# RWKV's 64x64 products issued alternately on four quarters of the array, the second head's inverse in the other half of the rows

## The reference

```
def step(S, inp):
    r_t, w_t, k_t, v_t, kk_t, a_t = inp
    sa = jnp.einsum('bhvk,bhk->bhv', S, -kk_t)
    S = (S * w_t[:, :, None, :] + sa[..., None] * (kk_t * a_t)[:, :, None, :]
         + v_t[..., None] * k_t[:, :, None, :])
    y = jnp.einsum('bhvk,bhk->bhv', S, r_t)
    return S, y
```

## Time and profile before

| | |
|---|---|
| median of 3 runs | 4763.44 us (4747.4, 4763.44, 4767.96) |
| the profiled execution | 4764.35 us, its span 4762.1 us |
| TensorE busy | 4174.8 us (88% of the span) |
| weight loads | 2744.4 us (58%) |
| VectorE, ScalarE, POOL busy | 1666.0, 1215.6, 700.7 us |
| mean granted clock of TensorE | 0.928 |

### The profile page before, as it was taken

One profiled execution on the slowest core, in us unless ns is written; L12 is line 12 of the kernel. 1 busy time (PEld: TensorE's weight loads), 2 busy tenths in 40 slices (PEclk: granted clock), 3 DMA queues, 4 the chain that ended last, 5 costly groups with the idle time before them and its releaser, 6 DMA issues. The chain is left out here.

```text
span 4762.1 us, 73074 instructions
## 1 busy us (share of the span) xinstructions
PE 4174.8 (88%) x28756; PEld 2744.4 (58%) x28756; DVE 1666.0 (35%) x2437; ACT 1215.6 (26%) x1719; POOL 700.7 (15%) x554
## 2 busy tenths in 40 slices
PE   6999669999896998599997979878889999999963
PEld 3888557777555886477774545533544444444423
DVE  3454743332233003643433323722341111111127
ACT  1111344342222111444332241611111111111104
POOL 2221012121112220022120110000001000010015
PEclk8999889899998999899998989989899999999985
DMA  6764232221423433222224315210149999999967
GB/s 221 240 198 154 83 119 83 93 68 64 159 89 115 132 115 104 93 87 71 98 66 147 106 49 214 84 47 27 65 185 359 359 354 358 360 362 360 356 242 264
DMA packets 292915, 803.45 MB, mean 169 GB/s; under 512 B 29121, under 2 KB 120770, under 8 KB 256834
## 3 DMA queue, kind: packets, MB, share of 16 engines
q1 hardware_dynamic: 244578, 624.80, 37.8%
q10 hardware_dynamic: 25632, 93.33, 4.9%
q0 software_dynamic: 22464, 81.80, 4.8%
HBM read 631.02 MB, written 168.82 MB: 168 GB/s over the span
## 5 line engine op out<-in xcount | busy, mean ns | idle before, releaser
L457 PE MATMUL ps<-s_proj_hS,s_proj_wS 128*128 128x512 f32 x3216 | 770.5, 402 | 62.9 <-POOL s_proj_wS L347 62.9
L457 PEld LDWEIGHTS ps<-s_proj_hS,s_proj_wS 128*128 128x128 f32 x3216 | 616.5, 192 | 213.1 <-ACT s_proj_wS L407 63.8
L1673 PE MATMUL ps<-gate_h,gate_w 128*128 128x512 f32 x1536 | 417.8, 416 | 2.5 <-ACT s_rw_og L1226 2.5
L3053 PE MATMUL ps<-s_exp_gu,keep_hT 128*128 128x512 f32 x736 | 339.6, 604 | 14.5 <-DMA s_exp_gu<-in_w_gu_dram 12.6
L1673 PEld LDWEIGHTS ps<-gate_h,gate_w 128*128 128x128 f32 x1536 | 284.1, 192 | 103.8 <-issue 42.0
L3037 PE MATMUL ps<-s_exp_wd,s_exp_aT 128*128 128x512 f32 x736 | 332.8, 595 | 1.9 <-ACT s_exp_aT L2963 1.9
L3058 PE MATMUL ps<-s_exp_gu,keep_hT 128*128 128x512 f32 x736 | 330.9, 592 | 0.0
L3003 DVE TENSOR_TENSOR s_exp_sg<-s_exp_sg,ps 128x256 f32<-128x256 f32 x92 | 38.7, 421 | 659.0 <-ACT s_exp_sg L2984 659.0
L1074 POOL TENSOR_TENSOR gate_w<-gate_raw,gate_w 128x512 fp32r<-128x512 f32 x128 | 168.7, 1319 | 652.5 <-ACT gate_w L1221 652.1
L347 POOL TENSOR_TENSOR s_proj_wS<-s_proj_w,s_proj_wS 128x1024 fp32r<-128x1024 f32 x67 | 170.7, 2550 | 572.9 <-ACT s_proj_wS L407 572.9
L2097 PE MATMUL ps<-keep_mix,s_mix_wb 128*128 128x512 f32 x512 | 224.9, 600 | 29.4 <-DMA s_mix_wb<-in_w_branch_rw_dram 28.5
(11 more groups left out here) (448 smaller groups left out, 6064.3 us busy)
## 6 DMA issues: line engine op xcount, KB each, us to landing
s_exp_gu<-in_w_gu_dram SPq DMA_DIRECT2D x184, 1024.0 KB, 10.8
s_exp_wd<-in_w_down_dram SPq DMA_DIRECT2D x92, 1024.0 KB, 8.8
yrow<-keep_hT ACTq DMA_DIRECT2D x92, 512.0 KB, 9.6
keep_mix<-in_w_ada_dram SPq DMA_DIRECT2D x80, 512.0 KB, 6.4
s_proj_w<-in_w_in_dram SPq DMA_DIRECT2D x66, 512.0 KB, 5.3
proj<-s_proj_o ACTq DMA_DIRECT2D x66, 512.0 KB, 2.7
gate_raw<-in_w_in_dram SPq DMA_DIRECT2D x128, 256.0 KB, 2.9
yrow<-keep_xT SPq DMA_DIRECT2D x4, 8192.0 KB, 49.1
```

The costliest lines, as they stand in the source:

```text
L457: mm = pe.matmul(k.ps[:, 6 + half if last else 2 * b + half, :], wS[:, b, x, t, :], hS[:, y, t, half * HALF:(half + 1) * HALF], start=(t = ...
L1673: mm = pe.matmul(k.ps[:, 7, :], wG[:, g % RING, w, t - y * HK, :], hG[:, h, t, :], start=(t == 0 and w + h == 0), stop=(t == KT - 1 and w ...
L3053: mm = pe.matmul(k.ps[:, 2 if u == 0 else 6, :], xT[:, u, t, :], gu[:, u, t, :], start=(t == 0), stop=False)
```

## The change

**The layout.** `cross(e, h)` is `rows(h ^ e)`: for the second head (e = 1) the other half of the partitions. XT, Y and MA of head 1 now lie there. X, LN, MP and ZX stay, so a level reads `rows(h)` and writes `cross(e, h)`, and the update of X and the product with Z read `cross(e, h)` and write `rows(h)`.

**The order.** Where a loop over heads stood outside, it now stands inside, so successive matmuls of `gram`, L, `level`, the update of X, masked scores by values and the product with Z alternate over all four quarters. The update of XT keeps its loops.

**What is added.** XT of head 1 can't start from LN any more, so B by A of that head is computed again into `cross(1, h)` of bank 2 (16 matmuls, semaphore `lx_ready`), after the first copy of X. `turn_a` becomes four 64x64 matmuls by the identity instead of one 128x128 transpose, per block.

**What is moved.** `gram` does both heads at once, Kd's second head too; the sums of the pair before go around it. VectorE copies X of both heads, then XT of both.

The diff, its core:

```diff
+        def cross(e, h):
+
+            return rows(h ^ e)
...
@@ -1453,18 +1456,26 @@
                 at = at_ts[:, n, :] if dst is X else at_st[:, NLV - n, :]
                 dve.copy_predicated(dst[:, e], at.unsqueeze(1).to_broadcast([P, NB, C]), src).then_inc(ready, 1)
 
-            def first_inverse(p, e):
+            def first_x(p, e):
                 dve.wait_ge(eye_ready, p + 1)
                 dve.wait_ge(l_ready, 2 * p + e + 1)
-                dve.wait_ge(pr_taken, 4 * p + e + 1)
                 put(X, 0, e, blocks(2 + e), x_ready)
-                put(XT, 0, e, LN[:, e, :, 0, :], xt_ready)
-
-            def level(p, n, e):
-                if n < NLV - 1:
+
+            def first_xt(p, e):
+                if e == 0:
+                    dve.wait_ge(pr_taken, 4 * p + 1)
+                    put(XT, 0, e, LN[:, e, :, 0, :], xt_ready)
+                else:
+                    dve.wait_ge(lx_ready, p + 1)
+                    put(XT, 0, e, blocks(2), xt_ready)
+
+            def level_x(p, n):
+                for e in range(2 if n < NLV - 1 else 0):
                     dve.wait_ge(dx_ready, (p * (NLV - 1) + n) * 2 + e + 1)
                     dve.wait_ge(x_ready, (p * NLV + n) * 2 + e + 1)
                     put(X, n + 1, e, blocks(4 + e), x_ready)
+
+            def level_xt(p, n, e):
                 dve.wait_ge(dxt_ready, (p * NLV + n) * 2 + e + 1)
                 dve.wait_ge(xt_ready, (p * (NLV + 1) + n) * 2 + e + 1)
                 put(XT, n + 1, e, blocks(2 + e), xt_ready)
@@ -1684,36 +1702,43 @@
                     tr = pe.transpose(k.ps[:, bank + c // 4, (c % 4) * P:(c % 4 + 1) * P], src(c), k.eye[:])
                 tr.then_inc(tr_ready, 1)
 
-            def gram(lhs, e, bank):
+            def gram(lhs, bank):
                 for c in range(NB):
                     for h in range(2):
-                        i = 2 * c + h
-                        mm = pe.matmul(k.ps[rows(h), bank + c // 4, (c % 4) * P:(c % 4 + 1) * P],
-                                       lhs[rows(e), i * C:(i + 1) * C], AR[rows(e), :, i * C:(i + 1) * C],
-                                       start=True, stop=True)
-                mm.then_inc(pr_ready, 1)
+                        for e in range(2):
+                            i = 2 * c + h
+                            mm = pe.matmul(k.ps[rows(h), bank[e] + c // 4, (c % 4) * P:(c % 4 + 1) * P],
+                                           lhs[rows(e), i * C:(i + 1) * C], AR[rows(e), :, i * C:(i + 1) * C],
+                                           start=True, stop=True)
+                            if c == NB - 1 and h:
+                                mm.then_inc(pr_ready, 1)
 
             def level(p, n):
                 for e in range(2):
                     pe.wait_ge(x_ready, (p * NLV + n) * 2 + e + 1)
                     if n:
                         pe.wait_ge(yy_taken, (p * NLV + n - 1) * 2 + e + 1)
-                    for c in range(NB):
-                        for h in range(2):
-                            mm = pe.matmul(k.ps[rows(h), e, c * C:(c + 1) * C], LN[rows(h), e, c, 0, :], X[rows(h), e, c, :],
+                for c in range(NB):
+                    for h in range(2):
+                        for e in range(2):
+                            mm = pe.matmul(k.ps[cross(e, h), e, c * C:(c + 1) * C], LN[rows(h), e, c, 0, :], X[rows(h), e, c, :],
                                            start=True, stop=True)
-                    mm.then_inc(yy_ready, 1)
+                            if c == NB - 1 and h:
+                                mm.then_inc(yy_ready, 1)
 
             def update(p, n):
                 for e in range(2):
                     pe.wait_ge(yy_taken, (p * NLV + n) * 2 + e + 1)
                     pe.wait_ge(xt_ready, (p * (NLV + 1) + n) * 2 + e + 1)
-                    if n < NLV - 1:
-                        for c in range(NB):
-                            for h in range(2):
-                                mm = pe.matmul(k.ps[rows(h), 4 + e, c * C:(c + 1) * C], XT[rows(h), e, c, :], Y[rows(h), e, c, :],
+                if n < NLV - 1:
+                    for c in range(NB):
+                        for h in range(2):
+                            for e in range(2):
+                                mm = pe.matmul(k.ps[rows(h), 4 + e, c * C:(c + 1) * C], XT[cross(e, h), e, c, :], Y[cross(e, h), e, c, :],
                                                start=True, stop=True)
-                        mm.then_inc(dx_ready, 1)
+                                if c == NB - 1 and h:
+                                    mm.then_inc(dx_ready, 1)
+                for e in range(2):
                     for c in range(NB):
                         for h in range(2):
                             mm = pe.matmul(k.ps[rows(h), 2 + e, c * C:(c + 1) * C], Y[rows(h), e, c, :], XT[rows(h), e, c, :],
@@ -1721,7 +1746,11 @@
                     mm.then_inc(dxt_ready, 1)
 
             def turn_a(q, c):
-                tr = pe.transpose(k.ps[:, c // 4, (c % 4) * P:(c % 4 + 1) * P], AR[:, 0, c * P:(c + 1) * P], k.eye[:])
+                for e in range(2):
+                    for h in range(2):
+                        i = 2 * c + h
+                        tr = pe.matmul(k.ps[cross(e, h), e, c * C:(c + 1) * C],
+                                       AR[rows(e), 0, i * C:(i + 1) * C], k.eye[rows(e), rows(e)], start=True, stop=True)
                 if c == NB - 1:
                     tr.then_inc(tr_ready, 1)
 
@@ -1768,35 +1797,43 @@
                     piece(g)
                 pe.wait_ge(ops_ready, p + 1)
                 pe.wait_ge(tr_taken, 4 * p + 2)
-                gram(B, 0, 4)
+                pe.wait_ge(tr_taken, 4 * p + 3)
+                gram(B, (4, 2))
                 if p:
                     means(p - 1, 0)
-                pe.wait_ge(tr_taken, 4 * p + 3)
-                gram(B, 1, 2)
+                if p % 2:
+                    piece(g + 1)
                 if p:
                     means(p - 1, 1)
-                if p % 2:
-                    piece(g + 1)
                 pe.wait_ge(tr_taken, 4 * p + 4)
-                gram(Kd, 0, 0)
+                pe.wait_ge(pr_taken, 4 * p + 1)
+                gram(Kd, (0, 4))
                 pe.wait_ge(pr_taken, 4 * p + 2)
-                for e in range(2):
-                    for c in range(NB):
-                        for h in range(2):
+                for c in range(NB):
+                    for h in range(2):
+                        for e in range(2):
                             i = 2 * c + h
                             mm = pe.matmul(k.ps[rows(h), 2 + e, c * C:(c + 1) * C], AR[rows(e), 0, i * C:(i + 1) * C],
                                            B[rows(e), i * C:(i + 1) * C], start=True, stop=True)
-                    mm.then_inc(l_ready, 1)
+                            if c == NB - 1 and h:
+                                mm.then_inc(l_ready, 1)
                 if p:
                     variances(p - 1, 0)
                 if p % 2:
                     piece(g + 2)
-                gram(Kd, 1, 4)
                 if p:
                     variances(p - 1, 1)
                 if p % 2:
                     piece(g + 3)
+                if p % 2:
                     g += 4
+                pe.wait_ge(x_ready, 2 * p * NLV + 1)
+                for c in range(NB):
+                    for h in range(2):
+                        i = 2 * c + h
+                        mm = pe.matmul(k.ps[cross(1, h), 2, c * C:(c + 1) * C], B[rows(1), i * C:(i + 1) * C], AR[rows(1), 0, i * C:(i + 1) * C],
+                                       start=True, stop=True)
+                mm.then_inc(lx_ready, 1)
                 pe.wait_ge(pr_taken, 4 * p + 3)
                 level(p, 0)
                 bonus_sums(p, 0)
@@ -1828,10 +1865,10 @@
                     pre_rate(p + 1, 0)
                 piece(g + 7)
                 level(p, 4)
-                for e in range(2):
-                    for c in range(NB):
-                        for h in range(2):
-                            mm = pe.matmul(k.ps[rows(h), 4 + e, c * C:(c + 1) * C], MP[rows(h), e, c, 0, :], Vt[rows(h), c, rows(e)],
+                for c in range(NB):
+                    for h in range(2):
+                        for e in range(2):
+                            mm = pe.matmul(k.ps[cross(e, h), 4 + e, c * C:(c + 1) * C], MP[rows(h), e, c, 0, :], Vt[rows(h), c, rows(e)],
                                            start=True, stop=True)
                 mm.then_inc(mv_ready, 1)
                 if more:
@@ -1844,11 +1881,13 @@
                 pe.wait_ge(mv_taken, p + 1)
                 for e in range(2):
                     pe.wait_ge(xt_ready, (p * (NLV + 1) + NLV) * 2 + e + 1)
-                    for c in range(NB):
-                        for h in range(2):
-                            mm = pe.matmul(k.ps[rows(h), 2 * e + c // 4, (c % 4) * P:(c % 4 + 1) * P], XT[rows(h), e, c, :],
```

(43 more changed lines are left out.)

4 lines of the change are left out of this document (2 added, 2 removed).

## The result

| | before | changed |
|---|---|---|
| median (runs of the first comparison) | 4755.42 us (4) | 4637.42 us (4; 4633.3 to 4643.57) |
| ratio to before, 95% interval | | 0.9758 [0.973, 0.9785] |
| again, later | | 0.973 [0.9706, 0.9754], 0.9745 [0.9717, 0.9772] |
| median of pooled runs | 4756.1 us (40) | 4635.0 us (14) |
| the profiled execution; its span | 4764.35; 4762.1 us | 4637.95; 4635.7 us |

The change makes the kernel 2.5% faster, 121 us by the pooled medians. (The 40 runs of the kernel before are those made beside the later experiments.

The account below looks back on a forecast made before the run. TensorE, busy 93%, was taken to bound the two RWKV stages, 1071 us. Gains from four-quarter order, less 3 us for transposes and 3 for instruction stalls, summed to 98 us: 4764.35 to 4666 us, range 4645 to 4714.

Parts of the forecast that it names:

- item 9: Updates, and level 4 with the group behind it: 128 passes may outrun their instructions; 3 us lost, bounds 0 and 15.
- Items 1 to 3: Levels 1 to 4, update of X, masked scores by values: 29.3 to 15.3 ns a pass; gains 28.5, 28.5, 7.1 us.
- Item 4: Product with Z: 3.64 us become 1.83 at 27 ns a pass; gain 14.4 us over 8 groups.
- The doubt about the bank: Levels and masked scores by values might keep 29 ns through same-bank order: 35.6 us less gain, 4702 us, chance 0.16.
- nothing overlaps: Old order within a level: passes alternate on two quarters writing one PSUM bank, at 29.3 ns each, without overlap.
- Item 5: Gram phase of the four odd pairs, with gate pieces: gain 4.1 us each after 0.5 off for shape changes, 16.4 in all.
- Item 6: Gram phase of even pairs, without pieces: pair 0 gains 0, pair 2 gains 3.1 in layer 1, 6 in layer 0; 9.1 together.
- if the clock rises at the same moment as before: Layer 0's pair 2 at half clock: 29.1 us become 20, half of the 9.1 lost again if so; 6 taken.
- Items 7 and 8: A's transposes as eight passes lose 3 us in scans with pieces; VectorE's copies of X and waits for Y cost nothing.
- The sum: 28.5 + 28.5 + 7.1 + 14.4 + 16.4 + 9.1 - 3 - 3 = 98 us of gain; chance 0.60 as it stands.
- The range: 4645 (no stalls, all 9.1 us of pair 2, 12 us of spread) to 4714 us (4702 to 4706 with 8 of spread).
- rival with the clock in it: Half clock in each of eight pairs, 4811 us, chance 0.03; or two or three more slow stretches, 4706 us, 0.06.

Follow-up runs that it names:

- level_eh: Changed kernel with a level's order putting `for e` outside `for h` within a block, so direct neighbours of different row halves write one bank; 4638.76 us, ratio 0.9746.
- before_again: The kernel before, unchanged, run again with a second profile; 4763.71 us, ratio 1.0012.
- nocross: Changed kernel's order of issue with the old layout, A turned by one transpose and no second L product of head 1; 4726.33 us, ratio 0.9942.
- level_heads: Changed kernel with the level's loop over heads put outside again, same layout and waits; 4669.7 us, ratio 0.9823.

## Why the prediction was right, and where it failed

The mechanism and the prices of the products held. Two steps failed, and both made the forecast too small: stops for instructions were priced as a loss only (item 9, 3 us forecast as a loss, 5.9 came as a gain), and the half clock was tied to one place and given no term for a gain (8 to 13 us, by the estimate above). Item by item:

- **Items 1 to 3** (levels, update of X, masked scores by values): 64.1 us forecast, 65.3 measured. The price of 15.3 ns from the earlier trace rows was exact.
- **Item 4**: 14.4 forecast, 13.9 measured; 128 columns take 28 ns a pass (1.90 less 0.1 over 64), not 27.
- **The doubt about the bank** was void: 15.3 ns in either order of banks. That the levels kept their gain I had put down to the halves shifting until each finds the other in the other bank. This isn't needed: level_eh, whose direct neighbours share a bank, takes the same time. What counts is how many quarters take turns, and here I was partly lucky: the price was right, the reason for it was not. The 29 ns of the earlier trace rows is two quarters' price, not one bank's. So two readings of the prediction were wrong: that in the old order "nothing overlaps" (one quarter alone takes 50 ns, so two in turn do overlap), and that this 29 ns agrees with the bank rule.
- **Item 5** (odd pairs): 4.1 forecast, 4.94 measured in each, 3.3 us in all. B, Kd and L gain 1.89, 1.89 and 0.75, as forecast, and the added products ate level 0's gain, as stated. What failed is the 0.5 us taken off for changes of shape: the joined groups save some, and 0.4 us came back instead.
- **Item 6** (even pairs): 9.1 forecast. At full clock pair 2 gives 3.4 and 2.7 for 2 x 3.1; pair 0 loses 0.2 in layer 0 and 1.4 in layer 1 (0.69 us of it a stop for instructions, the rest a level 0 at lower clock). That is 4.5 us; the other 16 of the measured 20.8 are the half-clock stretches that lay in this phase in the two profiles of before. The step that failed here is "if the clock rises at the same moment as before": it is tied to no such place, as before_again showed. I read a price of one execution as the program's. The sum was also loose: half of the 9.1 us would be 4.6, and I took 6.
- **Items 7 and 8**: -3 forecast, about -2 came: scans with pieces take some 0.3 us longer at full clock, 1.1 in layer 1's pair 0; the groups above show no wait for X's or Y's copies behind a piece (idle 0.0, and 1.1 us in all for a mask ahead of level 0).
- **Item 9** (instructions must arrive): -3 forecast, a gain of 5.9 measured in the stretch of the earlier trace rows. This is the step with the wrong sign. I counted only where shorter groups might run dry, and took the stops already there as fixed. They are not: first product to scan took 15.3 us in pair 0 and takes 12.2, though these products were not touched. The added instructions put other passes of the stretch at the 256-instruction steps. The gain repeats: without the piece, the eight stretches take 77.6 to 79.2 us in three profiles with the old order and 71.3 to 72.2 in seven of the new layout. In nocross, whose stops stand within eight instructions of where they were before, they take 74.2, so some 3.5 us or more come without the shift. How what is issued ahead makes the stops shorter is open.
- **The sum**: 1.2 more in items 1 to 3, 0.5 less in item 4, 3.3 more in item 5, 4.6 less in item 6, 1 more in item 7 and 8.9 more in item 9 turn 98 into 107. With 8 to 13 for the clock that is 115 to 120, of the 121 measured.
- **The range**: the terms named for its lower end (3 for stalls, 3.1 for pair 2, 12 of spread) give 4648 us, not 4645. It took 12 us of spread between runs but no gain from the clock, and no gain from stops. Every rival with the clock in it had it cost time. With 15 us for stops as the gain that mirrors the loss, and 12 for the clock beside the 12 of spread, its lower end would have been some 4627 us and held the result.

## What to carry to other kernels

Products of 64x64 are priced by how many quarters of the array take turns, so look for the layout that lets neighbours in the order of issue use all four, and change order and layout together: for a level, order alone gave nothing and layout alone 0.17 us of the 1.03. Only where the operands lay in four quarters already (the Gram products) was the order enough. Before a low clock is priced into one phase, look at a second execution; what lies at half clock in one profile is at full clock in the next. A stop for instructions is no property of its line. Here it stood at every 256th instruction, so anything added ahead moves it to other passes, and a change can shorten it as well as lengthen it. In these stretches a packet came at most every 3.2 us for 128 passes, by which a long row of passes shorter than some 25 ns outruns its instructions (an estimate from these traces). Long passes between the short ones took half of the stops or more out.

## What the runs showed of the hardware that was not expected

- Two quarters in turn are 1.7 times as fast as one, four 3.3 times: 50, 29 and 15.3 ns a pass of 64 columns. The turn must come with each product: level_heads uses all four quarters in a level, but two for its first half and two for its second, and takes 1.84 us.
- Sharing a bank between row halves costs nothing when their partitions differ: a level takes 0.98 us in either order of the banks.
- 8 stretches of 384 short passes stop for instructions 1.4 to 4.7 us each, always 256 instructions apart, and go on 1.05 to 1.61 us after a packet of 16384 bytes has landed. Twelve long passes of 0.25 us in their midst take some half of it out, and more when they are split.
- The same program has 30 us at half clock in one place in one execution and next to none there in the next.
